# A ninth and a tenth weight block held outside the ring of a mixture-of-experts stage: the tenth in a 2 MB buffer taken from the dynamic-DMA scratch, and one slot refilled in the middle of the output projection

## The chip, the core and the metric

The kernel runs on one core of one Trainium2 chip. The figure of merit is the device time of the program in microseconds (us), the median of repeated runs. TensorE is called PE in the rows, VectorE DVE, ScalarE ACT, GpSimd POOL and SyncE SP. "SPq" is SP's queue, from which most DMA transfers are issued.

## The reference, cut to what is computed

One decoder block on 256 tokens of width 1024, all in float32, ends in a mixture of 32 experts:

```python
h = rmsnorm(x, norm1_w[l])
proj = h @ w_in[l]                       # 1024 x 5632, nine parts
q_a, k_a, v_a, q_b, f_b, i_b, g_b, gate_a, gate_b = jnp.split(proj, IN_SPLITS, axis=-1)
y_a = moba_attention(rope(q_a), rope(k_a), v_a)
y_b = hgrn2(q_b, f_b, i_b, g_b, ...)
mixed = sigmoid(gate_a) * (y_a @ moba_up[l]) + sigmoid(gate_b) * (y_b @ hgrn_up[l])
x = x + mixed @ w_out[l]
h2 = rmsnorm(x, norm2_w[l])
# every expert e, on the tokens that were routed to it (top 4 of 32):
gu = xb @ w_gate_up[e] + b_gate_up[e]    # 1024 x 2048: 8 MB
y  = ((up + 1.0) * glu) @ w_down[e] + b_down[e]   # 1024 x 1024: 4 MB
x = x + sum of the weighted y
return rmsnorm(x, final_norm_w)
```

The weights of the experts are 32 times 12 MB. Every expert's weights are read once.

## The kernel before, in words

**The front part.** `w_in` comes in eleven blocks of 2 MB (FB, QB, QA, KA, VA, IB, ...), followed by `moba_up`, `hgrn_up` and the two halves of `w_out` (wo0, wo1). The list `LOADS` is that order, and SP issues it through a ring of `RING` = 3 places, which are the slots 5, 6 and 7 of the tile `S`. A place is filled again when PE is done with what it held: `filled(sp, name)` waits until PE has finished the unit `name`. Each block is split by ACT into a rounded part (`hi_a`, `hi_b`, `hi_c`, line 514) and by DVE or POOL into the rest (`w_lo`, line 352); PE multiplies with both. The block KA is split by ACT into `hi_b` and by POOL into `w_lo`. Of the output projection PE computes wo0 first, unsplit (units wo00 and wo10, line 1210), then wo1, split (units wo01 and wo11, lines 1260 to 1266).

**The expert part.** An expert is six blocks of 2 MB: four of `w_gate_up` (line 1476) and two of `w_down` (line 1516). Here they are numbered m = 0, 1, 2, ... through all experts, so block m is part m % 6 of expert m // 6: blocks 0 to 3 are gate and up of expert 0, blocks 4 and 5 its down part, blocks 6 to 9 gate and up of expert 1, blocks 10 and 11 its down part, block 18 the first of expert 3. In all there are 192. `S` has eight slots (`SLOTS` = 8). In the front part the slots are used for other things too, so they come free one by one, and SP puts blocks 0 to 7 into them in the order 0, 1, 2, 3, 5, 4, 6, 7. Block 8 does not go through `S`: it is held in four pieces of 512 KB (`KEPT` and three pages of the tile `M`, function `keep`). From block 9 on a block goes into slot (m - 1) % 8.

**What releases a load.** SP works through its queue in order. `used(q, m)` waits until PE has finished the block m of the group q of four experts. Ahead of the loop over groups stands

```python
            for m in range(SLOTS + 1, 24):
                used(0, m - SLOTS if m > 2 * SLOTS else m - SLOTS - 1)
                load(0, m)
```

so block 9 waits for the end of block 0, block 10 for block 1, up to block 16 for block 7 (a distance of nine), and from block 17 on every block waits for the one eight before it. The groups after the first have that distance of eight in `load_four`. The last block of all is loaded in two halves of 1 MB (line 435).

**PE's order in an expert.** Four gate and up blocks (16 matmuls each at line 1476, the fourth after the bias matmuls of line 1494), then the gather of the next pair (line 1447) or the combination of the last pair (line 1455; for the first expert line 1535), four transposes (line 1507), then the two down blocks (32 matmuls at line 1516). The end of the first 16 of these releases the slot of the first down block.

Of the kernel before, what the change touches and what calls it, by code (L numbers as in the profile page):

```python
# [11 lines left out]
P = 128  # L12
# [14 lines left out]
NEG = -1e30  # L27
BANKS = 8
SLOTS = 8
SCALE = DH ** -0.5  # L30
GROUP = 512
RING = 3

QA, KA, VA, QB, FB, IB, GB, GA0, GA1, GB0, GB1 = range(11)
# [78 lines left out]
def hybrid_block(nc, A, out):  # L113
    ctx = ExitStack()
    with ctx:
        def sb(name, shape, dt=F32):
            return ctx.enter_context(nc.sbuf_tensor(name, shape, dt))

        def sem(name):
            return ctx.enter_context(nc.semaphore(name))  # L120
# [33 lines left out]

        S = sb("S", [P, SLOTS, 4096])
        X = sb("X", [P, TT, D])
# [14 lines left out]
        SF = S[:].rearrange("p s n -> p (s n)")  # L171
        wr8 = [S[:, SLOTS - RING + s, :].rearrange("p (k n) -> p k n", k=KD) for s in range(RING)]
        wr4 = [S[:, SLOTS - RING + s, :].rearrange("p (k n) -> p k n", k=4) for s in range(RING)]

# [16 lines left out]
        def mpage(n, c=1):  # L191
            return M[:, 1024 * n:1024 * (n + c)]
# [30 lines left out]

        KEPT = sb("KEPT", [P, D])
        kept = [KEPT[:], mpage(10), mpage(5), mpage(6)]

        def h3(ap):
            return ap.rearrange("p (h t) -> p h t", h=GH)
# [78 lines left out]
        first_loaded, cst_loaded, router_loaded = sem("first_loaded"), sem("cst_loaded"), sem("router_loaded")  # L307

        slot_loaded = [sem(f"slot_loaded{s}") for s in range(SLOTS)]
        kept_loaded, last_loaded = sem("kept_loaded"), sem("last_loaded")  # L310

        weights_used = sem("weights_used")
        selw_ready = sem("selw_ready")
# [8 lines left out]
        def filled(eng, name):  # L322
            eng.wait_ge(bank_filled, AT_UNIT[name] + 1)

        def wait_drained(eng, name):
            who, n = drained(name)
            eng.wait_ge(drained_by[who], n)
# [15 lines left out]
        wgu = A["w_gate_up"].rearrange("l e (s p k) n -> (l e) s p (k n)", p=P, k=2)  # L343
        wdn = A["w_down"].rearrange("l e (h p c) n -> (l e) h p (c n)", p=P, c=4)
        gu_slot = [S[:, s, :].rearrange("p (k n) -> p k n", k=2) for s in range(SLOTS)]
        dn_slot = [S[:, s, :].rearrange("p (k n) -> p k n", k=4) for s in range(SLOTS)]

        def form_lo(eng, tensor_tensor, what, j):
# [9 lines left out]
        @block.sync  # L358
        def _(sp):
            for tt in range(TT):  # L360
                sp.dma_start(X[:, tt, :], A["x"][0, tt * P:(tt + 1) * P, :]).then_inc(x_loaded[tt], 16)
            sp.dma_start(CST[:, 0:128], A["cst"][:, 0:128]).then_inc(ident_loaded, 16)
            def load(e, m, slot=None):

                e, s, slot = e + m // 6, m % 6, (m - 1) % SLOTS if slot is None else slot
                src = wgu[e, s] if s < 4 else wdn[e, s - 4]
                if len(src.shape) == 3:
                    src = src[0]
                sp.dma_start(S[:, slot, :], src).then_inc(slot_loaded[slot], 16)

            def keep(k):
                sp.dma_start(kept[k], wgu[1, 2, :, 1024 * k:1024 * k + 1024]).then_inc(kept_loaded, 16)

            for n, what in enumerate(LOADS):
                if what == "mu":
                    keep(0)
                    filled(sp, "kT1")
                    load(0, 0, slot=0)
                if what == "wo0":
                    filled(sp, "ya1")  # L380
                    load(0, 1, slot=1)
                if n >= RING:
                    filled(sp, last_unit[LOADS[n - RING]])
                s = n % RING
                dst = wr4[s] if what in ("mu", "hu") else wr8[s]
                if n == 0:
                    sp.dma_start(dst[:, :, 0:256], load_src[what][:, :, 0:256]).then_inc(first_loaded, 16)
                    sp.dma_start(dst[:, :, 256:512], load_src[what][:, :, 256:512]).then_inc(w_loaded[s], 16)
                else:
                    sp.dma_start(dst, load_src[what]).then_inc(w_loaded[s], 16)  # L390
                if n == 1:
                    sp.dma_start(CST[:, 128:], A["cst"][:, 128:]).then_inc(cst_loaded, 16)
                    sp.dma_start(MSK[:], A["lmask"].rearrange("p (m t) -> p m t", t=CHUNK)).then_inc(lmask_loaded, 16)


            filled(sp, "hu3")
            for m in (2, 3, 5):
                load(0, m, slot=m)
            sp.wait_ge(mix_ready, 1)
            keep(1)  # L400
            filled(sp, "wo11")
            for m in (4, 6, 7):
                load(0, m, slot=m)
            wait_drained(sp, "rt")
            keep(2)
            keep(3)

            def used(q, m):

                i, s = q * 4 + m // 6, m % 6  # L410
                if s == 5:
                    sp.wait_ge(y_filled, i + 1)
                elif s == 3:
                    sp.wait_ge(gu_filled, i * 2 + 2)
                else:
                    sp.wait_ge(weights_used, i * 4 + min(s, 3) + 1)

            def load_four(q, e, stop=24):

                for m in range(stop):  # L420
                    used(q, m - SLOTS)
                    load(e, m)


            for m in range(SLOTS + 1, 24):
                used(0, m - SLOTS if m > 2 * SLOTS else m - SLOTS - 1)
                load(0, m)
            with sp.Fori(1, E // 4 - 1) as q:
                load_four(q, q * 4)

            load_four(E // 4 - 1, E - 4, stop=23)
            used(E // 4 - 1, 23 - SLOTS)
            last_slot = 22 % SLOTS
            for part, done in ((0, slot_loaded[last_slot]), (1, last_loaded)):
                sp.dma_start(S[:, last_slot, 2048 * part:2048 * part + 2048],
                             wdn[E - 1, 1, :, 2048 * part:2048 * part + 2048]).then_inc(done, 16)
            sp.wait_ge(rounds_ready, 1)
            most = sp.value_load(CMI[0:1, 0:1], min_val=0, max_val=T)
            with sp.If(most > CAP):
                with sp.Fori(1, ROUNDS) as r:  # L440
                    with sp.If(most > r * CAP):
                        with sp.Fori(0, E // 4) as q:
                            load_four(r * (E // 4) + q, q * 4)
# [35 lines left out]
        def _(se):  # L479
# [104 lines left out]
            def exps(h):  # L584
                se.wait_ge(smax_ready, h + 1)
                s = SM[:, h % 2, :]
                nc.scalar.activation(s[:, 0:128], s[:, 0:128], ACT.Exp, bias=nmx[:, 2 * h:2 * h + 1], scale=SCALE,
                                     accum_out=rsum[:, 2 * h:2 * h + 1])
                st.did(nc.scalar.activation(s[:, 128:384], s[:, 128:384], ACT.Exp, bias=nmx[:, 2 * h + 1:2 * h + 2],
                                            scale=SCALE, accum_out=rsum[:, 2 * h + 1:2 * h + 2]), exp_ready)  # L590

# [140 lines left out]
        def _(ve):  # L732
# [167 lines left out]
            def softmax_max(h):  # L900
# [8 lines left out]
                st.settle()  # L909
                st.did(v.tensor_scalar(nmx[:, 2 * h:2 * h + 2], mx, -SCALE, None, ALU.mult), smax_ready)  # L910

# [260 lines left out]
        def _(pe):  # L1172
# [285 lines left out]
            def arrived(q, m, opening):  # L1458

                if opening and m == SLOTS:  # L1460
                    pe.wait_ge(kept_loaded, 64)
                    return None
                slot, before = (m, 0) if opening and m < SLOTS else ((m - 1) % SLOTS, q * 3 + (m - 1) // SLOTS)
                pe.wait_ge(slot_loaded[slot], before * 16 + 16)
                return slot

# [163 lines left out]
```

## Time and profile before

| | us |
|---|---|
| median of 3 runs | 1179.83 |
| lowest and highest of them | 1179.66, 1180.95 |
| the profiled execution, its own time | 1182.38 |
| the profiled execution, its span | 1180.2 |

The span counts from the first to the last recorded instruction; the profiled execution's own time holds 2.18 us more that lie around it. The traces give instants within the span. PE is busy for 1075.2 us of the span (91%), DVE for 345.7, ACT for 213.7, POOL for 62.4. DMA moved 438.88 MB at a mean of 372 GB/s.

### The profile page before, as it was taken

How to read it: one execution, taken by the hardware profiler on the slowest of the kernel's cores; microseconds unless marked ns; L12 is line 12 of the kernel's file. 1: busy time of each engine (PE TensorE's matmuls, PEld its weight loads, DVE VectorE, ACT ScalarE, POOL GpSimd, SP SyncE). 2: the span in 40 equal slices, each digit the busy share in tenths (PEclk: the TensorE clock that was granted, in tenths of full speed). 3: DMA queues.
4: the chain of work that ended last, by engine and by line, in shares of the span. 5: the costliest groups of instructions: out<-in, count | busy, mean ns of one | idle time of the engine just before them, and what ended most of it. 6: DMA issues, size and time to landing. Idle time of an engine off the chain costs nothing.

```text
span 1180.2 us, 13741 instructions
## 1 busy us (share of the span) xinstructions
PE 1075.2 (91%) x5571; PEld 518.0 (44%) x5571; DVE 345.7 (29%) x646; ACT 213.7 (18%) x338; POOL 62.4 (5%) x39
## 2 busy tenths in 40 slices
PE   7988999999999999998989898989898989898896
PEld 6867999643343434332323232323233323233332
DVE  4896648532211111111111111111111111111113
ACT  4632646300101111010101010101010101010102
POOL 0491003000000000000000000000000000000000
PEclk9998999999999999999999999999999999999999
DMA  8542556899999999999999999999999999999992
GB/s 280 212 144 72 194 186 215 287 385 401 395 428 427 426 429 428 428 428 430 428 428 428 428 430 428 428 428 429 429 428 429 428 429 428 428 428 429 427 425 117
DMA packets 46794, 438.88 MB, mean 372 GB/s; under 512 B 4852, under 2 KB 7176, under 8 KB 22184
## 3 DMA queue, kind: packets, MB, share of 16 engines
q1 hardware_dynamic: 44560, 435.99, 88.9%
q10 hardware_dynamic: 2200, 2.39, 0.6%
q8 instruction: 27, 0.44, 0.2%
q14 instruction: 7, 0.06, 0.0%
HBM read 437.32 MB, written 1.05 MB: 371 GB/s over the span
## 4 chain that ended last, share of the span: by engine, by line
PE 50%; DMA 42%; POOL 3%; DVE 3%; issue 1%; ACT 1%; DVEq 0%; SPq 0%; ACTq 0%; POOLq 0%
DMA S<-in_w_gate_up_dram 40%; PE PS L1476 17%; PE PS L1516 11%; PE PS L1247 7%; PE PS L1447 3%; PE PS L1455 2%; PE PS L1210 1%; DVE M L1106 1%; PE PS L1201 1%; POOL w_lo L352 1%; PE PS L1263 1%; POOL S L469 1%; DMA S<-in_w_in_dram 1%; POOL S L468 1%; PE PS L1266 1%
## 5 line engine op out<-in xcount | busy, mean ns | idle before, releaser
L1476 PE MATMUL PS<-S,M 128*64 128x512 f32 x2032 | 458.0, 596 | 45.1 <-DMA S<-in_w_gate_up_dram 44.4
L1476 PEld LDWEIGHTS PS<-S,M 128*64 128x64 f32 x2032 | 139.1, 137 | 343.0 <-issue 249.9
L1516 PE MATMUL PS<-S,M 128*64 128x512 f32 x1024 | 228.5, 599 | 27.5 <-DVE M L1106 27.5
L1092 DVE TENSOR_SCALAR M<-PS 128x256 f32<-128x256 f32 x64 | 27.0, 423 | 692.6 <-PE PS L1476 692.6
L1516 PEld LDWEIGHTS PS<-S,M 128*64 128x64 f32 x1024 | 71.1, 137 | 164.3 <-issue 129.2
L679 ACT ACTIVATE M<-M 128x256 f32<-128x256 f32 x64 | 26.7, 417 | 489.4 <-DVE M L1092 489.4
L684 ACT COPY M<-PS 64x512 f32<-64x512 f32 x32 | 18.5, 578 | 336.5 <-PE PS L1516 336.5
L1447 PE MATMUL PS<-M,XN 128*128 128x128 f32 x512 | 59.8, 275 | 0.0
L1447 PEld LDWEIGHTS PS<-M,XN 128*128 128x128 f32 x512 | 58.5, 192 | 0.5 <-issue 0.2
L1455 PE MATMUL PS<-M 128*128 128x512 f32 x120 | 55.5, 605 | 0.0
L352 DVE TENSOR_TENSOR w_lo<-S,hi_a 128x2048 fp32r<-128x2048 f32 (+1 forms) x20 | 42.2, 2127 | 6.1 <-ACT hi_a L514 6.0
L514 ACT CAST hi_a<-S 128x2048 fp32r<-128x2048 f32 (+1 forms) x24 | 38.4, 1623 | 9.1 <-DMA S<-in_w_out_dram 6.8
L1100 DVE TENSOR_TENSOR M<-M 128x256 f32<-128x256 f32 x64 | 38.8, 607 | 2.3
L1455 PEld LDWEIGHTS PS<-M 128*128 128x128 f32 x120 | 21.6, 189 | 33.7 <-issue 33.7
L1247 PE MATMUL PS<-hT_hi,w_lo 128*128 128x256 f32 x208 | 29.2, 283 | 0.0
L1083 DVE TENSOR_TENSOR M<-PS,SMALL 128x512 f32<-128x512 f32 x32 | 22.1, 692 | 21.4 <-PE PS L1447 21.4
L1096 DVE SCALAR_TENSOR_TENSOR M<-M 128x256 f32<-128x256 f32 x64 | 27.2, 425 | 2.2
L1106 DVE COPY M<-PS 128x512 f32<-128x512 f32 x32 | 22.0, 686 | 17.4 <-PE PS L1507 17.4
L1247 PEld LDWEIGHTS PS<-hT_hi,w_lo 128*128 128x128 f32 x208 | 26.8, 192 | 0.0
L1094 DVE TENSOR_SCALAR M<-PS 128x256 f32<-128x256 f32 x64 | 26.6, 415 | 0.0
L1263 PE MATMUL PS<-w_lo,hT_hi 128*128 128x512 f32 x64 | 17.6, 422 | 7.6 <-POOL w_lo L352 7.6
L1494 PE MATMUL PS<-bias_parts,pick 128*128 128x512 f32 x64 | 23.5, 448 | 0.0
(241 smaller groups left out, 829.9 us busy)
## 6 DMA issues: line engine op xcount, KB each, us to landing
S<-in_w_gate_up_dram SPq DMA_DIRECT2D x127, 2048.0 KB, 32.6
S<-in_w_down_dram SPq DMA_DIRECT2D x63, 2048.0 KB, 35.3
S<-in_w_in_dram SPq DMA_DIRECT2D x10, 2048.0 KB, 8.2
S<-in_w_out_dram SPq DMA_DIRECT2D x2, 2048.0 KB, 7.8
S<-in_w_in_dram SPq DMA_DIRECT2D x2, 1024.0 KB, 9.2
S<-in_moba_up_dram SPq DMA_DIRECT2D x1, 2048.0 KB, 7.7
S<-in_hgrn_up_dram SPq DMA_DIRECT2D x1, 2048.0 KB, 7.9
S<-in_w_down_dram SPq DMA_DIRECT2D x2, 1024.0 KB, 34.1
```

The lines of the kernel that those rows point to most:

```text
L352: tensor_tensor(raw_part(what, j, lo=True), raw_part(what, j), hi_part(PIECES[n][3]), ALU.subtract).then_inc(lo_ready[PIECES[n][2]], 1)
L514: st.did(nc.scalar.copy(hi_part(PIECES[n][3]), raw_part(what, j)), hi_ready)
L1092: v.tensor_scalar(gate[:, c], g2[:, :, 0], LIMIT, None, ALU.min).then_inc(gate_ready, 1)
L1096: v.scalar_tensor_tensor(out=up[:, c], in0=up[:, c], scalar=1.0, in1=gate[:, c], op0=ALU.add, op1=ALU.mult).then_inc(up_ready, 1)
L1100: v.tensor_tensor(act.rearrange("p (c q) -> p q c", c=4)[:, 64 * half:64 * half + 64, :], up[:, c].rearrange("p (q c) -> p q c", c=4), sg[ ...
L1106: v.tensor_copy(actT, multi[:].rearrange("p (c s) -> p c s", c=4)).then_inc(actT_ready, 1)
L1247: ins = mm(ps[:, T * a:T * a + T], w[:, k, P * a:P * a + P], x[:, k, :], start=(k == 0 and w is w_h and x is hi), stop=(k == kn - 1 and x ...
L1263: mm(ps[:], hi[:, k, rows], w_l[:, k, :], start=False, stop=False)
L1447: ins = mm(dst[:, P * a:P * a + P], XN[:, tt, P * k:P * k + P], sel[:, tt, :], start=(tt == 0), stop=(tt == TT - 1))
L1455: mm(acc[tt][n][:], selT[:, P * tt:P * tt + P], Y[:, 512 * n:512 * n + 512], start=False, stop=True, skip_group_check=True)
L1476: ins = mm(gu[half][64 * g:64 * g + 64, :], hTe[:, k, tok], w, start=(k == 0), stop=(k == KD - 1))
L1516: ins = mm(multi[64 * n:64 * n + 64, :], actT[:, k, 64 * kh:64 * kh + 64], dn_slot[slot][:, k, 512 * n:512 * n + 512], start=(kh == 0 and ...
```

## The change

The change adds a tile `EXTRA` of one block (16 KB on each of 128 partitions). Room for it is made by the argument `dynamic_dma_scratch_size=1024` of the program's constructor, where it had its default. `EXTRA` takes block 9 (the fourth gate and up block of expert 1). It is loaded once, early in the front part: SP issues it directly ahead of its wait for the slot of KA. Blocks 10 to 17 then wait for the block ten before them, and from block 18 on the distance is eight, as it was from block 17 on. Block m goes into slot (m - 2) % 8. Apart from that, block 6 is loaded into slot 6 as soon as PE has finished the unit wo10, and no longer with blocks 4 and 7 after wo11.

```diff
@@ sizes and tiles
 SLOTS = 8
+AHEAD = 2
 ...
         kept = [KEPT[:], mpage(10), mpage(5), mpage(6)]
+        EXTRA = sb("EXTRA", [P, 4096])
@@ SP: load(), and the loads of the front part
-                e, s, slot = e + m // 6, m % 6, (m - 1) % SLOTS if slot is None else slot
+                e, s, slot = e + m // 6, m % 6, (m - AHEAD) % SLOTS if slot is None else slot
 ...
             for n, what in enumerate(LOADS):
+                if what == KA:
+                    sp.dma_start(EXTRA[:], wgu[1, 3]).then_inc(extra_loaded, 16)
                 if what == "mu":
@@ SP: the slots that come free with the output projection
             keep(1)
+            filled(sp, "wo10")
+            load(0, 6, slot=6)
             filled(sp, "wo11")
-            for m in (4, 6, 7):
+            for m in (4, 7):
                 load(0, m, slot=m)
@@ SP: the first group of experts
-            for m in range(SLOTS + 1, 24):
-                used(0, m - SLOTS if m > 2 * SLOTS else m - SLOTS - 1)
+            for m in range(SLOTS + AHEAD, 24):
+                used(0, m - SLOTS if m >= 2 * SLOTS + AHEAD else m - SLOTS - AHEAD)
                 load(0, m)
@@ PE: arrived()
+                if opening and m == SLOTS + 1:
+                    pe.wait_ge(extra_loaded, 16)
+                    return -1
-                slot, before = (m, 0) if opening and m < SLOTS else ((m - 1) % SLOTS, q * 3 + (m - 1) // SLOTS)
+                slot, before = (m, 0) if opening and m < SLOTS else ((m - AHEAD) % SLOTS, q * 3 + (m - AHEAD) // SLOTS)
@@ the program
-    nc = _bacc.Bacc("TRN2", target_bir_lowering=False, num_devices=1)
+    nc = _bacc.Bacc("TRN2", target_bir_lowering=False, num_devices=1, dynamic_dma_scratch_size=1024)
```

SP's queue in the kernel before, from the start of the program to the first block that waits for a slot of the expert part (`bank_filled` counts PE's finished units, `drained_by_dve` the units that DVE has read, `weights_used`, `gu_filled` and `y_filled` PE's finished blocks):

```order
8 L390 DMA S<-in_w_in_dram 128x8x512
9 L390 DMA S<-in_w_in_dram 128x8x512 [waits bank_filled] x8
...
18 L369 DMA S<-in_w_down_dram 128x4096
19 L372 DMA M<-in_w_gate_up_dram 128x1024 [waits mix_ready]
20 L369 DMA S<-in_w_down_dram 128x4096 [waits bank_filled]
21 L369 DMA S<-in_w_gate_up_dram 128x4096 x2
22 L372 DMA M<-in_w_gate_up_dram 128x1024 [waits drained_by_dve]
23 L372 DMA M<-in_w_gate_up_dram 128x1024
24 L369 DMA S<-in_w_gate_up_dram 128x4096 [waits weights_used]
```

The same stretch of the changed kernel's SP queue:

```order
8 L395 DMA S<-in_w_in_dram 128x8x512
9 L379 DMA EXTRA<-in_w_gate_up_dram 128x4096
10 L395 DMA S<-in_w_in_dram 128x8x512 [waits bank_filled] x8
...
20 L375 DMA M<-in_w_gate_up_dram 128x1024 [waits mix_ready]
21 L372 DMA S<-in_w_gate_up_dram 128x4096 [waits bank_filled]
22 L372 DMA S<-in_w_down_dram 128x4096 [waits bank_filled]
23 L372 DMA S<-in_w_gate_up_dram 128x4096
24 L375 DMA M<-in_w_gate_up_dram 128x1024 [waits drained_by_dve]
25 L375 DMA M<-in_w_gate_up_dram 128x1024
```

A load of 4096 elements per partition is new between QA (the row ahead of it) and KA (the first of the eight behind it), and block 6 has a wait of its own ahead of block 4's.

SP's queue in the first group of experts, before. The first row is block 12; then come 13 (`weights_used`), 14 (`y_filled`), 15, 16, 17 (`gu_filled`), 18 (`weights_used`) and 19 (`y_filled`):

```order
26 L369 DMA S<-in_w_gate_up_dram 128x4096 [waits gu_filled]
27 L369 DMA S<-in_w_gate_up_dram 128x4096 [waits weights_used]
28 L369 DMA S<-in_w_gate_up_dram 128x4096 [waits y_filled]
29 L369 DMA S<-in_w_gate_up_dram 128x4096 [waits weights_used]
30 L369 DMA S<-in_w_down_dram 128x4096 [waits weights_used]
31 L369 DMA S<-in_w_down_dram 128x4096 [waits gu_filled]
32 L369 DMA S<-in_w_gate_up_dram 128x4096 [waits weights_used]
33 L369 DMA S<-in_w_gate_up_dram 128x4096 [waits y_filled]
```

The same queue after, from block 13 (`gu_filled`) on: 14 (`weights_used`), 15 (`y_filled`), 16 and 17 (`weights_used`), 18 (`weights_used`), 19 (`y_filled`):

```order
28 L372 DMA S<-in_w_gate_up_dram 128x4096 [waits gu_filled]
29 L372 DMA S<-in_w_gate_up_dram 128x4096 [waits weights_used]
30 L372 DMA S<-in_w_gate_up_dram 128x4096 [waits y_filled]
31 L372 DMA S<-in_w_down_dram 128x4096 [waits weights_used] x2
32 L372 DMA S<-in_w_gate_up_dram 128x4096 [waits weights_used]
33 L372 DMA S<-in_w_gate_up_dram 128x4096 [waits y_filled]
```

What each wait released up to block 16 now releases the block after it; block 17 has moved from the end of block 9 to the end of block 7; the rows of blocks 18 and 19, and all behind them, stand as they were.

## Rows read from the trace of the kernel before

**Rows 1.** The page, part 2: PE's busy tenths and DMA's GB/s in 40 slices

```profile
PE   7988999999999999998989898989898989898896
...
GB/s 280 212 144 72 194 186 215 287 385 401 395 428 427 426 429 428 428 428 430 428 428 428 428 430 428 428 428 429 429 428 429 428 429 428 428 428 429 427 425 117
```

**Rows 2.** Windows of 60 us: busy (count) by engine, PEclk, DMA share, GB/s

```profile
360.00:420.00 60.00, 58.27 (x278) 22.29 (x276) 10.86 (x26) 6.80 (x11) 0.00 (x0) 1.00 1.01 428
...
1080.00:1140.00 60.00, 52.87 (x250) 19.91 (x248) 10.52 (x25) 5.64 (x10) 0.00 (x0) 1.00 1.01 427
```

**Rows 3.** The chain that ended last, in order of time: start, us, what

```profile
27.93 8.30 DMA S<-in_w_in_dram
36.26 3.71 ACT hi_b L514 x2
...
84.59 9.40 POOL w_lo L352 x2
...
298.12 7.09 PE PS L1516 x32
...
526.02 34.23 DMA S<-in_w_gate_up_dram
```

**Rows 4.** Windows from 301 to 360 us, as rows 2

```profile
301.00:302.00 1.00, 1.00 (x6) 0.29 (x4) 0.00 (x0) 0.00 (x0) 0.00 (x0) 1.00 0.16 66
302.00:303.00 1.00, 1.00 (x8) 0.40 (x6) 0.00 (x0) 0.00 (x0) 0.00 (x0) 1.00 0.97 197
303.00:304.00 1.00, 1.00 (x8) 0.32 (x6) 0.00 (x0) 0.00 (x0) 0.00 (x0) 1.00 0.55 115
304.00:305.00 1.00, 1.00 (x6) 0.29 (x4) 0.00 (x0) 0.00 (x0) 0.00 (x0) 1.00 0.79 328
305.00:360.00 55.00, 53.27 (x256) 20.75 (x254) 10.85 (x26) 6.91 (x13) 0.00 (x0) 1.00 1.01 429
```

**Rows 5.** SP's issues in time: start, us from first to last of the row

```profile
253.40 0.33 SPq L369 DMA_DIRECT2D S<-in_w_gate_up_dram  x1
256.83 3.76 SPq L369 DMA_DIRECT2D S<-in_w_down_dram  x2
264.51 17.54 SPq L369 DMA_DIRECT2D S<-in_w_gate_up_dram  x4
285.16 8.01 SPq L369 DMA_DIRECT2D S<-in_w_down_dram  x2
301.81 10.63 SPq L369 DMA_DIRECT2D S<-in_w_gate_up_dram  x4
```

**Rows 6.** Windows 274:278 and 278:301, as rows 2

```profile
274.00:278.00 4.00, 4.00 (x20) 1.29 (x18) 0.00 (x0) 0.00 (x0) 0.00 (x0) 1.00 0.70 229
278.00:301.00 23.00, 22.05 (x120) 9.93 (x118) 5.55 (x12) 2.37 (x5) 0.00 (x0) 1.00 1.00 427
```

**Rows 7.** Windows from 25 to 36 us, as rows 2

```profile
25.00:29.00 4.00, 4.00 (x36) 4.00 (x35) 2.33 (x3) 1.06 (x2) 0.00 (x0) 1.00 0.03 7
29.00:30.00 1.00, 1.00 (x10) 1.00 (x10) 0.96 (x4) 1.00 (x1) 0.00 (x0) 1.00 0.80 133
...
35.00:36.00 1.00, 1.00 (x10) 1.00 (x10) 1.00 (x2) 0.00 (x0) 0.00 (x0) 1.00 0.18 66
```

**Rows 8.** Waits between 20 and 110 us: total, times, longest

```profile
PE PS L1263 <- POOL w_lo L352: 7.6, 1, 7.6
...
ACT hi_b L514 <- DMA S<-in_w_in_dram: 1.8, 1, 1.8
```

**Rows 9.** The window 232:234, as rows 2

```profile
232.00:234.00 2.00, 1.70 (x12) 1.29 (x10) 1.10 (x3) 0.22 (x1) 0.00 (x0) 1.00 0.30 59
```

**Rows 10.** PE's timeline: the down part of expert 0

```profile
269.46 8.78 PE L1516 MATMUL PS<-S,M 128*64 128x512 f32 x32 [0.78 <-DVE M L1106]
```

**Rows 11.** The window 271:272, as rows 2

```profile
271.00:272.00 1.00, 1.00 (x4) 0.24 (x2) 0.00 (x0) 0.00 (x0) 0.00 (x0) 0.50 0.92 393
```

**Rows 12.** The page, part 3: the DMA queue of SP: packets, MB, share

```profile
q1 hardware_dynamic: 44560, 435.99, 88.9%
```

More of the change, by code:

```diff
@@ L309, in hybrid_block @@
         slot_loaded = [sem(f"slot_loaded{s}") for s in range(SLOTS)]
-        kept_loaded, last_loaded = sem("kept_loaded"), sem("last_loaded")
+        kept_loaded, last_loaded, extra_loaded = sem("kept_loaded"), sem("last_loaded"), sem("extra_loaded")
         weights_used = sem("weights_used")
@@ L345, in hybrid_block @@
         gu_slot = [S[:, s, :].rearrange("p (k n) -> p k n", k=2) for s in range(SLOTS)]
+        gu_slot.append(EXTRA[:].rearrange("p (k n) -> p k n", k=2))
         dn_slot = [S[:, s, :].rearrange("p (k n) -> p k n", k=4) for s in range(SLOTS)]
@@ L432, in _ @@
             used(E // 4 - 1, 23 - SLOTS)
-            last_slot = 22 % SLOTS
+            last_slot = (23 - AHEAD) % SLOTS
             for part, done in ((0, slot_loaded[last_slot]), (1, last_loaded)):
```

## The prediction, made before the changed kernel ran

> **What bounds the kernel now.** I read the page's 40 slices first. From the twelfth slice on (324 us) to the last but one, DMA moves 425 to 430 GB/s in every slice [rows 1], and the windows of 60 us say the same, at a DMA share of 1.0 [rows 2]. So the back of the kernel is a stream of 2 MB blocks, and its end is the start of the unbroken stream plus the bytes that are left. A block is 2.097 MB, and at 428 GB/s it takes 4.90 us. The chain that ended last agrees in its back half: it runs over DMA from 526 us on [rows 3].
>
> The front is another thing. There the GB/s fall as low as 72 [rows 1], and the chain runs over PE, POOL, ACT and once over a transfer [rows 3]. So the question is where the unbroken stream starts, and on what. The reader is to look for the last pause of DMA: it lies at 301 to 305 us, where the four windows of 1 us carry 66, 197, 115 and 328 GB/s in place of 428 [rows 4]. What they miss is (4 x 428 - 706) / 428 = 2.35 us. Behind it the windows are full [rows 2, 4]. SP issues nothing between 293.2 us (block 17, the end of its row: 285.16 + 8.01) and 301.81 us, and the issue at 301.81 is block 18 [rows 5]. It waits for the end of block 10, which is the first half of the down matmuls that PE starts at 298.12 and that take 7.09 us for both halves [rows 3]: 298.12 + 3.55 = 301.67. That is the instant on which the end of the kernel hangs. Check: 174 blocks (18 to 191) x 4.90 = 852.6 us, from about 303 us (issue plus the ramp of rows 4) gives 1155.6, and the last 25 us of the span are the last expert's down part, the final norm and the stores.
>
> **The change, part by part.**
>
> *Blocks 10 to 17 wait for a block further back.* Each is asked for as early as the block before it was. The last two pauses of DMA tell what that is worth. In 274 to 278 us the windows miss 4 x (1 - 229/428) = 1.86 us, where the load waits for the end of block 4; between the two pauses, from 278 to 301 us, DMA is full [rows 6], and moves five blocks (13 to 17). With the change block 14 takes the place of block 13 behind the first pause, so that only four blocks (14 to 17) are left, and the stream runs dry about 4.9 us earlier, near 296 us. Block 17's own issue moves to the end of block 7, 285 us, and is no hindrance. But block 18 still waits for the end of block 10, and PE comes there no earlier: it does not wait for DMA anywhere from 249 to 526 us (the chain stays on PE and DVE [rows 3]). So the pause ahead of block 18 grows from 2.35 to 2.35 + 4.90 = 7.25 us, and the 4.9 us are given back in full. Gain: 0. If the stream did depend on bytes alone here, it would be 4.90 us; both ends are kept.
>
> *The distance behind block 17.* It is eight before and after, for every later block; the same blocks in the same order. 0.
>
> *Block 6 at wo10.* DMA has a hole at 232 to 234 us, 59 GB/s [rows 9], and block 6 now fills it, so that the loads ahead of the expert part are done some 2 to 3 us earlier. What is late next is again a release: block 10 is asked for at 253.40 as block 9 was [rows 5]. 0. On SP's queue the new wait stands ahead of blocks 4, 7 and two pieces of block 8, all of which wait for later instants anyway. 0.
>
> *EXTRA ahead of KA.* This load is on a path. The chain holds the load of KA, issued at 27.93 and landed 8.30 us later, then ACT's split of it at 36.26 [rows 3], for which ACT stood still for 1.8 us [rows 8]. From there it goes on through ACT, DVE and POOL to POOL's `w_lo` at 84.59 [rows 3], for which PE waits 7.6 us [rows 8], and PE is then the chain up to block 10. So what KA loses arrives at 301.81 in full. EXTRA is issued behind QA, and QA's bytes are through by 25 us but for 28 KB (7 GB/s over 25 to 29); then DMA idles until KA's first bytes at about 29.1 us (133 GB/s in 29 to 30 [rows 7]). That is a pause of 4.1 us at most, 3.8 if I give the stragglers 0.3 us. EXTRA needs 4.90 us at the stream's rate. KA is then late by 0 (if engines that are through with QA before 25 us start EXTRA at once) to 1.1 us (4.9 - 3.8). I take 0.6, near the middle, since the sixteen engines do not end together and each begins its part by itself. If EXTRA went no faster than KA does, which needs from 29.1 to 35.2 us [rows 7], it would be 6.1 - 3.8 = 2.3 us. That is the outer bound.
>
> A rule of the Trainium skill speaks against this place. "DMA: Bandwidth & Descriptors", section "Where 436 GB/s comes from", says that for HBM to SBUF the memory side binds, at about 358 GB/s per core (it also shows 425 for one core alone). By 358 GB/s a block would be 5.9 us, and EXTRA would hold KA back by 2.1 us. The trace disagrees: 428 GB/s [rows 2].
>
> *The scratch cut to 1 KB.* SP's loads, 435.99 MB of the 438.88, go by a queue of the kind hardware_dynamic, and the page lists no software queue [rows 12]. Nothing that runs here used the room, so 0. All tiles lie 15 KB lower, at the same alignment to 1 KB: 0.
>
> *PE's instructions* are the same in number, shape and order; 16 of them read EXTRA in place of `S`. 0.
>
> **Sum.** 0 + 0 + 0 + 0.6 us. The profiled execution has a span of 1180.2 and a time of its own of 1182.38, so the changed one should show a span of 1180.8 beside about 1183.0. The median of before is 1179.83, 2.55 us under the profiled time; with the same 0.6 it becomes 1180.4.
>
> **What blurs it.** PE's clock falls to its lower level now and then: in 271 to 272 us the granted share is 0.50 (1.2 GHz) [rows 11], and the down part of expert 0 that lies there takes 8.78 us [rows 10] where that of expert 1 takes 7.09 [rows 3]. That is 1.69 us on the way to block 10, after a stretch of small matmuls. With everything shifted by 0.6 us it may fall away or come again elsewhere, so plus or minus 1.7 is possible without any meaning. The three runs of before already spread over 1.29 us.
>
> **The rivals.**
>
> *A, my forecast:* the pause ahead of block 18 takes back the gain; +0.6. Its own range is 1178.7 (the slow clock gone: 0.6 - 1.7) to 1182.1 (EXTRA at its outer bound, 2.3). Chance 0.77.
>
> *B, the block is gained.* One block less in the stream: 1179.83 - 4.90 + 0.6 = 1175.5. For it speaks that DMA is full for 850 us, and that any byte moved ahead of the stream shortens it. Against it, that the bytes were never what block 18 waited for, since DMA is empty when it is asked for [rows 4]. It would need PE at block 10 some 5 us earlier. Chance 0.11.
>
> *C, slower: KA is held back by more than 2.4 us.* The place is the load of KA at 27.93 us, which now has EXTRA in front of it in the same queue, and ACT, DVE, POOL and then PE wait behind it. It decides from 2.4 us on (0.2%), that is, if EXTRA takes over 6.2 us; KA itself takes 8.30 us from issue to landing [rows 3], but it is cut into rows of 2 KB and EXTRA into rows of 16 KB. At 1 us beyond the outer bound the time is 1179.83 + 3.3 = 1183.1. Chance 0.12.
>
> **How the numbers follow.** A difference of 0.2% (2.4 us) is about what a measurement of this kernel tells from none. Faster is B, 0.11; slower is C, 0.12; the same is A, 0.77. The likeliest is A: 1180.4. To leave out no more than 2 in 10 I reach a little past A's own range on both sides, to 1177.6 and to 1182.9, so that part of C is within.
>
> **What would show it.** Right: the windows ahead of 302 us show DMA nearly empty for about 7 us from 295 or 296 on, and full before; SP issues block 17 near 285 to 286 us and block 18 at 301.8 plus the delay of KA, 302 to 303; the GB/s behind that are 428 again, to the same end. Block 10 is issued near 253.4 and the hole at 232 is gone. EXTRA lands by about 30 us, KA at 36.3 to 37.4, ACT's wait for KA grows from 1.8 to between 2 and 3 us, and PE's wait for POOL's `w_lo` from 7.6 by as much. Wrong: block 18 issued before 300 us, or a chain that enters DMA earlier than 526 us with a shorter span (B); or a landing of KA past 38.6 us (C). The prediction is also wrong if PE at block 10 waits for something that I hold for hidden, a matmul of expert 0 or 1 on a late block, since that moves the one instant on which all hangs.

## The result, and the profile after

| | before | after |
|---|---|---|
| median, same runs | 1181.54 us (9 runs, 1178.95 to 1183.35) | 1183.3 us (9 runs, 1181.28 to 1184.98) |
| ratio | | 1.002, 95% interval [1.0011, 1.003] |
| the profiled execution, its own time | 1182.38 us | 1184.98 us |
| its span | 1180.2 us | 1182.7 us |

The change makes the kernel slower by 0.2%, which is 2.4 us (1.3 to 3.5). The median of the kernel before over nine runs is 1.7 us above the one of three runs that the prediction started from, so the times are compared by their ratio.

The back of the kernel first, as in [rows 1]. DMA's GB/s in 40 slices, of the kernel after:

```profile
GB/s 351 210 144 72 190 189 214 332 339 400 326 426 429 427 428 428 427 429 429 427 429 429 427 429 429 427 429 429 427 429 429 427 429 429 427 429 428 427 426 88
```

The stream is the same from the twelfth slice on. In the first slice there is more (351 against 280: EXTRA is there), and in the eleventh less (326 against 395). Windows around the last pause, kernel after (us, then busy and count of PE, PEld, DVE, ACT, POOL, then PEclk, DMA share, GB/s; they answer to [rows 4, 6]):

```profile
278.00:290.00 12.00, 12.00 (x58) 3.96 (x56) 0.00 (x0) 1.16 (x2) 0.00 (x0) 1.00 0.99 423
...
296.00:298.00 2.00, 1.82 (x17) 1.58 (x15) 0.91 (x2) 0.00 (x0) 0.00 (x0) 1.00 0.44 180
298.00:300.00 2.00, 1.24 (x6) 0.48 (x8) 0.71 (x2) 0.00 (x0) 0.00 (x0) 1.00 0.04 16
300.00:302.00 2.00, 2.00 (x12) 0.72 (x10) 0.00 (x0) 0.00 (x0) 0.00 (x0) 1.00 0.00 0
302.00:304.00 2.00, 2.00 (x12) 0.61 (x10) 0.00 (x0) 0.00 (x0) 0.00 (x0) 1.00 0.60 123
304.00:306.00 2.00, 2.00 (x12) 0.69 (x10) 0.00 (x0) 0.10 (x1) 0.00 (x0) 1.00 0.72 262
306.00:360.00 54.00, 52.27 (x252) 20.33 (x250) 10.85 (x26) 6.18 (x12) 0.00 (x0) 1.00 1.01 430
```

From 296 to 306 us DMA moves 2 x (180 + 16 + 0 + 123 + 262) = 1162 GB/s x us where 4280 would fit, so it misses 3118 / 428 = 7.29 us. Before, the pause was 2.35 us. The block that EXTRA took out of the stream has become 4.9 us of idle DMA. SP's issues show why (start, us from first to last of the row; they answer to [rows 5]):

```profile
10.70 6.01 SPq L379 DMA_DIRECT2D EXTRA<-in_w_gate_up_dram  x1
25.27 112.81 SPq L395 DMA_DIRECT2D S<-in_w_in_dram  x8
...
254.04 3.76 SPq L372 DMA_DIRECT2D S<-in_w_down_dram  x2
260.90 18.36 SPq L372 DMA_DIRECT2D S<-in_w_gate_up_dram  x4
282.37 3.76 SPq L372 DMA_DIRECT2D S<-in_w_down_dram  x2
302.46 10.63 SPq L372 DMA_DIRECT2D S<-in_w_gate_up_dram  x4
```

Block 17, the end of the row at 282.37, is issued at 286.1 us and no longer at 293.2, but block 18 at 302.46, 0.65 us later than before, since it waits for the same block 10.

Now the front. The chain that ended last, of the kernel after (start, us, what; it answers to [rows 3]):

```profile
25.27 11.64 DMA S<-in_w_in_dram
36.94 3.72 ACT hi_b L521 x2
...
85.24 9.37 POOL w_lo L355 x2
94.66 3.78 PE PS L1270 x8
...
298.76 7.09 PE PS L1526 x32
```

The load of KA takes 11.64 us from issue to landing where it took 8.30. It was issued 2.66 us earlier (25.27 against 27.93), since PE ended the unit f1 earlier in this execution, and nevertheless landed 0.7 us later. ACT's wait for it, of the kernel after, and PE's for POOL (total, times, longest; [rows 8]):

```profile
PE PS L1270 <- POOL w_lo L355: 9.9, 2, 9.1
...
ACT hi_b L521 <- DMA S<-in_w_in_dram: 5.2, 1, 5.2
```

ACT stands still for 5.2 us where it was 1.8. The windows of that place, kernel after (as above; [rows 7]), show no pause between QA, EXTRA and KA:

```profile
25.00:26.00 1.00, 1.00 (x11) 1.00 (x10) 0.09 (x1) 0.72 (x2) 0.00 (x0) 1.00 0.99 410
...
29.00:30.00 1.00, 1.00 (x11) 1.00 (x9) 1.00 (x1) 1.00 (x2) 0.00 (x0) 1.00 0.88 348
...
34.00:35.00 1.00, 1.00 (x11) 1.00 (x10) 1.00 (x2) 0.00 (x0) 0.00 (x0) 1.00 0.66 242
35.00:36.00 1.00, 1.00 (x11) 1.00 (x9) 0.23 (x1) 0.00 (x0) 0.00 (x0) 1.00 0.08 29
36.00:37.00 1.00, 1.00 (x9) 0.96 (x8) 0.00 (x0) 0.06 (x1) 0.00 (x0) 1.00 0.03 12
```

DMA works without a gap into the 35th us. As long as it does, KA's bytes can't be through earlier, whenever in this stretch it is asked for. The last 41 KB trickle in over two more microseconds, at a share of DMA of 0.08 and 0.03, which is about one engine of the sixteen or less. EXTRA itself landed 21.0 us after its issue, at 31.7 us.

**The two profiled executions differ by 2.5 us of span, and only 0.65 of it is in this place.** The last expert's down part starts at 1156.97 us in the changed kernel and at 1155.85 in the one before, 1.12 us later, so 0.5 us came in along the stream. The remaining 1.4 us lie behind it, in the final combination. Windows of the tail, kernel before:

```profile
1171.00:1176.00 5.00, 2.07 (x5) 0.57 (x3) 4.06 (x7) 3.74 (x12) 0.00 (x0) 0.99 0.00 0
```

The same window, kernel after:

```profile
1171.00:1176.00 5.00, 4.74 (x7) 1.52 (x5) 1.51 (x3) 1.93 (x6) 0.00 (x0) 0.58 0.00 0
```

PE's clock is at its lower level for more of that window (granted share 0.58 against 0.99). From the start of the last down part to the end of the span the ten profiled executions of the table below take between 22.6 us (e5) and 25.7 (after). The changed kernel's is the longest, and e2 with 25.4 the next, while e8, which has EXTRA at the same place, takes 24.5 and lies among the others. No run was made to find out what sets this stretch, so its 1.4 us stay unexplained.

### The profile page after: what moved, and what is told of

Its sections match the earlier page's. It is cut to its first block, busy times and chain, and to the rows that moved or that the text cites. A ratio compares the mean times of both kernels' runs of the same rounds, so it can differ in the third digit from the quotient of the medians.

```text
span 1182.7 us, 13735 instructions
## 1 busy us (share of the span) xinstructions
PE 1074.9 (91%) x5571; PEld 517.3 (44%) x5571; DVE 345.6 (29%) x646; ACT 213.8 (18%) x338; POOL 62.3 (5%) x39
## 4 chain that ended last, share of the span: by engine, by line
PE 50%; DMA 42%; POOL 3%; DVE 3%; issue 1%; ACT 1%; DVEq 0%; SPq 0%; ACTq 0%; POOLq 0%
DMA S<-in_w_gate_up_dram 40%; PE PS L1486 17%; PE PS L1526 11%; PE PS L1254 7%; PE PS L1454 3%; PE PS L1462 2%; PE PS L1217 1%; DVE M L1113 1%; DMA S<-in_w_in_dram 1%; POOL w_lo L355 1%; PE PS L1270 1%; POOL S L476 1%; POOL S L475 1%; PE PS L1273 1%; PE PS L1208 1%
```

## The experiments

Every experiment is compared with runs of the kernel before that stand beside it: 29 runs with a median of 1181.45 us for e1 to e4, and 35 with a median of 1180.14 for e5 to e8. The ratios are estimated from all runs of both kernels, and so can differ a little from the ratio of the two medians.

**Theory T1:** the loss is the load of KA behind EXTRA, and its price is not a constant: KA can't land before about 36.9 us, so the price is 36.9 less the instant at which it would have landed, which depends on how early PE ends f1 (the unit whose end frees KA's place) in that execution. **T2:** the memory's layout, the scratch or the new waits cost it. **T3:** the tenth block gained its 4.9 us, and the late KA or something else ate them and more. **T4** (for e5): any 2 MB load in this stretch costs the front something.

**e1: EXTRA's load put into a long pause.**

```diff
-                if what == KA:
+                if what == GA1:
                     sp.dma_start(EXTRA[:], wgu[1, 3]).then_inc(extra_loaded, 16)
```

> The changed kernel with one edit: EXTRA is loaded ahead of the wait for GA1's place (DMA is idle there from about 86 to 108 us) and no longer ahead of KA's. Theory T1 (the loss is KA's load, which stands behind EXTRA in SP's queue and can't land before about 36.9 us, however early PE asks for it): KA lands about 8.3 us after its issue again, and the time is that of the kernel before within 0.15%, 1.5 to 3 us below the changed kernel; no gain, since block 18 still waits for block 10. Rival T2 (the loss comes from the shifted tiles, the scratch or the new waits and their order): it stays 0.2% slower than the kernel before. Rival T3 (the tenth block's 4.9 us are a real gain that the late KA ate up): 0.3 to 0.4% faster than the kernel before.

Measured: 1181.3 us against 1181.45, ratio 0.9997 [0.9985, 1.0009]. The loss is gone, and nothing is gained. EXTRA was issued at 76.0 us here and landed at 88.4, in a stretch behind which DMA idles until 105 us. ACT's split of KA in e1 (start, us):

```profile
34.24 3.71 ACT L521 CAST hi_b<-S 128x2048 fp32r<-128x2048 f32 x2 [1.72 <-DMA S<-in_w_in_dram]
```

KA was issued at 26.01 and read at 34.24. DMA's last pause in e1:

```profile
294.00:296.00 2.00, 1.30 (x12) 1.06 (x11) 1.10 (x2) 0.00 (x0) 0.00 (x0) 1.00 0.13 49
296.00:298.00 2.00, 1.75 (x8) 0.63 (x10) 0.19 (x1) 0.00 (x0) 0.00 (x0) 1.00 0.00 0
298.00:300.00 2.00, 2.00 (x12) 0.72 (x10) 0.00 (x0) 0.00 (x0) 0.00 (x0) 1.00 0.00 0
300.00:302.00 2.00, 2.00 (x12) 0.70 (x10) 0.00 (x0) 0.00 (x0) 0.00 (x0) 1.00 0.72 139
```

Here too some 7 us are missing. T2 and T3 fall.

**e2: the kernel before, with EXTRA loaded ahead of KA and read by nobody.**

```diff
+        EXTRA = sb("EXTRA", [P, 4096])
...
+                if what == KA:
+                    sp.dma_start(EXTRA[:], wgu[1, 3]).then_inc(extra_loaded, 16)
```

(and the scratch cut to 1 KB). It moves 2 MB that it does not use.

> The kernel before, with the tile EXTRA, the scratch cut, and EXTRA's load ahead of KA's wait, but nobody reads EXTRA: block 9 and all others are loaded and released as in the kernel before (2 MB more are moved). T1: slower than before by as much as the changed kernel, 1.5 to 2.5 us. T2 with the waits and the refill of block 6 as its cause: as fast as before. T3: slower than the changed kernel by 4.9 us.

Measured: 1183.81 against 1181.45, ratio 1.002 [1.0011, 1.0029], the changed kernel's own ratio. The load alone, at this place, is the whole loss. ACT's split of KA in e2:

```profile
36.85 1.91 ACT L517 CAST hi_b<-S 128x2048 fp32r<-128x2048 f32 x1 [4.68 <-DMA S<-in_w_in_dram]
```

**e3: the scratch cut and the tile allocated, nothing else.**

```diff
+        EXTRA = sb("EXTRA", [P, 4096])
-    nc = _bacc.Bacc("TRN2", target_bir_lowering=False, num_devices=1)
+    nc = _bacc.Bacc("TRN2", target_bir_lowering=False, num_devices=1, dynamic_dma_scratch_size=1024)
```

> The kernel before with the scratch cut to 1 KB and the tile EXTRA allocated, never loaded nor read. T1 and T3: as fast as the kernel before within 0.1%. T2 with the memory's layout as its cause: slower by 1.5 to 2.5 us.

Measured: 1179.82 us against 1181.45, ratio 0.9993 [0.9983, 1.0003]. The smaller scratch and the lower tiles cost nothing that can be measured, as the prediction had it.

**e4: e1, and EXTRA used a second time, for block 18.**

```diff
+            for m in range(SLOTS + AHEAD, 2 * SLOTS + AHEAD):
+                used(0, m - SLOTS - AHEAD)
+                load(0, m, slot=m - SLOTS - AHEAD)
+            used(0, 9)
+            sp.dma_start(EXTRA[:], wgu[3, 0]).then_inc(extra_loaded, 16)
+            for m in range(2 * SLOTS + AHEAD + 1, 24):
+                used(0, m - SLOTS - 1)
+                load(0, m)
+            for m in range(24):
+                used(1, m - SLOTS - (m < 3))
+                load(4, m)
...
```

The diff stands against the changed kernel and is cut: the rows that it replaces, and PE's side of the same numbering, are left out. The second group of experts is taken out of the loop, and from block 19 on a block goes into slot (m - 3) % 8.

> As e1, and EXTRA is used a second time: block 18 goes into it when block 9 has been used, so that block 18 waits for block 9 (at about 293 us) and not for block 10 (302 us), and the blocks 19 to 26 wait for the block nine before them. My account of the pause (block 18 waits for the end of block 10, and all bytes behind it follow) forecasts that the pause ahead of block 18 is gone and that the stream ends 4.9 us earlier: 0.35 to 0.45% faster than the kernel before, about 1175 where that one takes 1180. Rival (the end hangs on the bytes or on the memory's rate and not on that release): the time of e1.

Measured: 1176.17 against 1181.45, ratio 0.9951 [0.9936, 0.9965], over six runs of e4: by the ratio 5.8 us faster (4.1 to 7.6), the forecast 4.9 within it. SP's issues in e4:

```profile
280.70 3.76 SPq L372 DMA_DIRECT2D S<-in_w_down_dram  x2
291.81 0.33 SPq L436 DMA_DIRECT2D EXTRA<-in_w_gate_up_dram  x1
300.78 7.20 SPq L372 DMA_DIRECT2D S<-in_w_gate_up_dram  x3
```

and its windows:

```profile
296.00:298.00 2.00, 1.06 (x7) 0.34 (x7) 1.03 (x2) 0.00 (x0) 0.00 (x0) 1.00 1.01 426
298.00:300.00 2.00, 2.00 (x12) 0.72 (x10) 0.00 (x0) 0.00 (x0) 0.00 (x0) 1.00 0.96 410
300.00:302.00 2.00, 2.00 (x12) 0.71 (x10) 0.00 (x0) 0.00 (x0) 0.00 (x0) 1.00 0.75 156
302.00:304.00 2.00, 2.00 (x12) 0.58 (x9) 0.00 (x0) 0.00 (x0) 0.00 (x0) 1.00 0.57 188
```

Block 18 goes out at 291.81, DMA is busy up to 300 us, and the pause of 2.5 us that remains ((8 x 428 - 2360) / 428 over the four windows) now stands ahead of block 19, which is what waits for block 10 at 300.78. One block fewer comes behind that instant. That is the gain that the change was one wait short of, and the rival, that the end hangs on the bytes alone, falls.

**e5: EXTRA's load ahead of VA's wait**, that is, behind KA on SP's queue.

```diff
-                if what == KA:
+                if what == VA:
```

> The changed kernel with EXTRA's load ahead of VA's wait, one place later on SP's queue (behind KA's issue). EXTRA is then in front of VA as it was in front of KA. T1 (what costs is that ACT and all behind it wait for KA): KA lands 8.3 us after its issue, VA lands up to 2 us later than it did, and nobody waits for VA, so the time is that of the kernel before within 0.15%. Rival T4 (any 2 MB among the loads of this part holds the front back, through the memory's rate or the queue): slower by 0.1 to 0.2%, as with EXTRA ahead of KA.

Measured: 1179.79 against 1180.14, ratio 0.9996 [0.9984, 1.0008]. VA's load landed 9.1 us after its issue in e5, 0.2 more than before's 8.9, and ACT took it up without a wait:

```profile
53.37 3.73 ACT L521 CAST hi_a<-S 128x2048 fp32r<-128x2048 f32 x2
```

VA was held back by hardly anything, less than the 2 us that I allowed for, so this run does not tell whether a late VA would be free; it tells that 2 MB in this stretch cost nothing when KA is ahead of them. T4 falls.

**e6: 1 MB of EXTRA ahead of KA, 1 MB ahead of GA1.**

```diff
+                if what in (KA, GA1):
+                    c = slice(0, 2048) if what == KA else slice(2048, 4096)
+                    sp.dma_start(EXTRA[:, c], wgu[1, 3, :, c]).then_inc(extra_loaded, 16)
```

> The changed kernel with only the first 1 MB of EXTRA ahead of KA and the second ahead of GA1. T1 (the price is the part of the transfer that does not fit between the end of QA's bytes at about 25 us and KA's first ones, 1.3 us after PE's unit f1): 2.45 us have to fit in place of 4.9, KA is late by 0 to 1.2 us according to how early f1 ends, and the time is 0 to 0.7 us above the kernel before, at least 1 us below the changed kernel. Rival (a fixed price for a load that stands there, a straggling DMA engine for instance): as slow as the changed kernel.

Measured: 1181.55 against 1180.14, ratio 1.0008 [0.9997, 1.0019]. The middle lies between none and 2 MB, where T1 wants it, but the interval touches both the kernel before and the changed one, so this run settles nothing by itself. In its profiled execution KA was issued at 27.21 and read 7.8 us later, not held back: this was one of the executions with a late PE, in which 1 MB fits into the pause.

**e7: only the early refill of slot 6**, in the kernel before.

```diff
+            filled(sp, "wo10")
+            load(0, 6, slot=6)
             filled(sp, "wo11")
-            for m in (4, 6, 7):
+            for m in (4, 7):
```

> The kernel before with block 6 loaded at the end of wo10 and nothing else. T1: within 0.1% of the kernel before; DMA's hole at 232 to 234 us is filled and the pause ahead of block 9 is longer by as much. Rival (T2, the refill disturbs the small loads of the router or the biases): slower by some 0.1%.

Measured: ratio 1.0003 [0.9989, 1.0018]. Windows of e7:

```profile
232.00:234.00 2.00, 1.69 (x16) 1.67 (x16) 1.72 (x5) 1.89 (x4) 0.00 (x0) 1.00 0.93 393
...
246.00:250.00 4.00, 4.00 (x26) 2.28 (x27) 1.20 (x2) 0.05 (x1) 0.00 (x0) 1.00 0.22 85
```

The hole of [rows 9] is filled (393 GB/s), and DMA is nearly idle from 246 us on (85 GB/s up to 250), until block 9 is asked for at 251.19. Up to 220 us this program is the kernel before, and its profiled execution shows what that kernel does when PE is early: KA issued at 25.67 and read at 33.53:

```profile
25.67 11.89 SPq L390 DMA_DIRECT2D S<-in_w_in_dram  x2
```

```profile
33.53 3.72 ACT L516 CAST hi_b<-S 128x2048 fp32r<-128x2048 f32 x2 [1.35 <-DMA S<-in_w_in_dram]
```

**e8: e4 with EXTRA's first load ahead of KA again** (the edit of e4 on the changed kernel).

> As e4 (EXTRA used for blocks 9 and 18, distance nine up to block 26), but with EXTRA's first load ahead of KA. If the two effects are independent, the 1.5 to 2.5 us of KA and the gain of 4.9 us add: about 0.2 to 0.3% faster than the kernel before, 2 us behind e4. Rival (the late KA costs nothing once the stream starts on a release of its own): as fast as e4.

Measured: 1177.41 against 1180.14, ratio 0.9972 [0.996, 0.9984]. The two effects add: e4's ratio of 0.9951 and the 0.002 of the changed kernel make 0.9971.

**All profiled executions side by side** (us; from the same views as above):

| execution | f0 on PE: us | KA issued | KA read by ACT | PE goes on behind POOL's `w_lo` | block 18 issued | down part of the last expert | end of the span |
|---|---|---|---|---|---|---|---|
| before | 9.53 | 27.93 | 36.26 | 94.03 | 301.81 | 1155.85 | 1180.2 |
| e3 (room only) | 9.39 | 27.83 | 35.87 | 93.60 | 299.80 | 1154.49 | 1179.0 |
| e1 (EXTRA at GA1) | 7.17 | 26.01 | 34.24 | 91.98 | 299.94 | 1154.54 | 1179.2 |
| e7 (refill only) | 7.17 | 25.67 | 33.53 | 91.53 | 297.90 | 1152.35 | 1177.3 |
| e5 (EXTRA at VA) | 7.17 | 25.51 | 33.45 | 91.19 | 297.35 | 1151.72 | 1174.3 |
| e4 (EXTRA at GA1, twice) | 8.86 | 27.32 | 35.53 | 93.30 | 291.81, block 19: 300.78 | 1150.49 | 1174.8 |
| e6 (half of EXTRA at KA) | 8.97 | 27.21 | 35.02 | 93.05 | 300.68 | 1155.12 | 1179.2 |
| after (EXTRA at KA) | 7.17 | 25.27 | 36.94 | 94.66 | 302.46 | 1156.97 | 1182.7 |
| e2 (EXTRA at KA, dead) | 7.17 | 25.66 | 36.85 | 94.56 | 301.06 | 1155.42 | 1180.8 |
| e8 (EXTRA at KA, twice) | 7.17 | 25.92 | 36.83 | 94.54 | 292.16, block 19: 301.14 | 1151.15 | 1175.6 |

Three things are to be read off. Without the whole of EXTRA in front, KA is read 7.8 to 8.3 us after its issue, between 33.45 and 36.26 us; with it, in all three executions, between 36.83 and 36.94. PE goes on 57.7 to 58.0 us after that in every row. And the last expert's down part starts 854.0 to 854.7 us after the issue of block 18, in the rows where block 18 waits for block 10 (849.7 and 850.0 us after that of block 19 in e4 and e8, one block of 4.9 us less). The mean of KA's reading is 34.81 us in the six rows without EXTRA in front and 36.87 in the three with it. The difference, 2.06 us, lies within the loss that was measured (2.4 us, 1.3 to 3.5). All three executions with EXTRA in front happen to be ones with an early PE, KA asked for by 25.92 us. That KA is read at 36.9 in one with a late PE too, and costs only 0.6 to 0.7 us there, is what T1 says, and no profile shows it.

The timed runs speak for it. The eleven runs of e2 lie between 1182.97 and 1185.24 us, the 29 of the kernel before beside them between 1178.9 and 1183.91: the fastest has become 4.1 us slower and the slowest 1.3. A fixed price would be expected to move both about alike.

## Why the prediction was wrong

*The back of the kernel came out as predicted.* The pause ahead of block 18 was to grow from 2.35 to 7.25 us and measured 7.29; the release of block 10 as the instant on which the end hangs is shown by e4 and by the constant 854 us; the refill at wo10, the scratch and the layout were put at 0 and measured 1.0003 and 0.9993. KA as the load on the path, with its full delay arriving at block 18, was right as well: +0.7 us at ACT, +0.65 at block 18 in the profiled pair.

*The step that failed is the size of the term "EXTRA ahead of KA": "I take 0.6", with 2.3 as the outer bound.* The mechanism was right, the term was mis-sized: it measured 2.06 us in the mean over the profiled executions (six without EXTRA in front, three with it), 2.4 us (1.3 to 3.5) in the timed runs. I took the pause that EXTRA had to fit into, 3.8 us, from one execution, in which PE ended f1 at 27.9 us. In others it ends at 25.5, the pause is then 1.4 us, and EXTRA, with its 4.9 us, takes away all that an early PE would have given: up to 36.9 - 33.5 = 3.4 us. What I held for a constant, the instant at which KA is asked for, varies by 2.7 us over the ten executions (25.27 to 27.93), and the added load clips that variation from one side. For an execution with PE as late as in the one that I read, T1 gives 36.9 - 36.3 = 0.6 us, my own number.

The signs that the prediction named show the same. KA landed between 36.3 and 37.4 us, block 17 was issued at 286.1 and block 18 at 302.46, as forecast. But ACT's wait for KA grew to 5.2 us and not to between 2 and 3, PE's wait for `w_lo` grew by 1.5 us and not by as much as ACT's, and EXTRA landed at 31.7 us and not by 30.

*Why PE is early or late:* both kernels compute f0 with the same 32 matmuls at the same place. PE in the kernel before (start, us):

```profile
12.63 9.53 PE L1201 MATMUL PS<-M,S 128*128 128x256 f32 x32 [0.78 <-DVE M L758]
```

and in the kernel after:

```profile
12.32 7.17 PE L1208 MATMUL PS<-M,S 128*128 128x256 f32 x32 [0.78 <-DVE M L765]
```

KA is issued 5.8 us behind the end of f0 in all ten executions, so f0's time, 7.17 to 9.53 us, carries nearly the whole variation. It does not go with EXTRA: f0 took 7.17 us in e1, e5 and e7 without EXTRA in front, and 8.97 in e6 with half of it there. Window 13 to 17 us of the kernel before:

```profile
13.00:17.00 4.00, 4.00 (x10) 3.16 (x10) 2.42 (x3) 3.98 (x3) 0.00 (x0) 1.00 1.06 389
```

and of the kernel after:

```profile
13.00:17.00 4.00, 4.00 (x21) 3.51 (x20) 2.70 (x4) 3.98 (x3) 0.00 (x0) 1.00 1.06 389
```

Ten matmuls of 128x256 in one, 21 in the other. The ratio is that of TensorE's two clock levels, 1.2 and 2.4 GHz. The granted clock reads 1.00 in both windows, so that the rows don't show it, and that it is the clock stays an inference.

*Rival C named this mechanism* and had 0.12. Its deciding point was put wrongly: "if EXTRA takes over 6.2 us", a landing of KA "past 38.6 us". EXTRA's bytes kept to the rate that I had assumed but for little (410 to 426 GB/s from 25 to 29 us), and KA landed at 36.9, well before 38.6. It was the other end of the interval that moved. Rival B, the gain of a block, did not occur; e4 shows that it needed one release more. The figure of 358 GB/s for HBM to SBUF (the Trainium skill, "DMA: Bandwidth & Descriptors", "Where 436 GB/s comes from"), by which KA would have been late by an estimated 2.1 us, hits the measured size by accident. The traces disagree with it as a bound here: the stream runs at 426 to 430 GB/s after as before.

*The predicted time* of 1180.4 us and its range to 1182.9 also started from a median of three runs that lay 1.7 us below the one of nine. Of the 2.9 us by which the measured median of 1183.3 lies above the forecast, 1.7 are this start and 1.2 the term (the two medians of nine are 1.8 us apart, less 0.6).

## What to carry to other kernels

An added prefetch only shortens a DMA-bound stretch if the release that starts the stretch moves too: find the last pause of DMA, see which block is issued at its end and what that block waits for, and check that the edit changes this very wait. Here one more use of the same buffer (block 18) turned the changed kernel's +0.2% into -0.3% (e8), and with EXTRA's load out of KA's way 0.0% into -0.5% (e1 and e4). And a pause of DMA in one profile is not room: a load put in front of one that an engine waits for has to fit into the pause of the earliest execution, or go behind it, which cost nothing (e5) on the same queue 15 us later.

## What the runs showed of the hardware

The issue of EXTRA held SP's queue for 6.01 us (at 10.70 us, right behind the issues of QB, the constants and QA), where the same instruction takes 0.33 us in the expert part (e4, at 291.81), and 0.58 us at 25.93 in e5. In e6 half of EXTRA, 1 MB, held it as long (6.00 us, at 11.11). Nothing waited behind it here; a load that is due sooner behind such an issue would be held back by it.

PE's clock fell to its lower level about the down part of expert 0 in some executions and not in others (granted share 0.50 in 270 to 272 us before, 1.00 in e3). That part took 8.78 us (before, after, e4, e6), 8.49 (e2), 8.53 (e8), 10.10 (e1) or 7.09 (e3, e5, e7). Block 18 follows only in part. It is issued 206.2 to 206.4 us behind PE's restart where the part took 7.09 us, 207.6 to 208.0 behind it where it took 8.78 or 10.10, and 206.5 in e2; in e1, e2 and e8 the stretch ahead of the part was about 1 us shorter (174.3 to 174.5 us against 175.1 to 175.7), and why is open. So three stretches vary from execution to execution: f0 (7.17 to 9.53 us), this one, and the end of the kernel (22.6 to 25.7 us). Single runs of the kernel before lie 5 us apart in one set (1178.9 to 1183.91) and 7.4 in the other (1176.6 to 1183.99), which is more than the change is worth; how much of it each of the three gives was not separated.
